# Sixteen norm roots taken with tokens on the partitions, in a two-block transformer on one Trainium2 core

## The reference

```python
def rms_norm(x, g):
    xf = x.astype(jnp.float32)
    y = xf * lax.rsqrt(jnp.mean(xf * xf, axis=-1, keepdims=True) + EPS)
    return (y * g.astype(jnp.float32)).astype(x.dtype)
```

```python
    x = x + rms_norm(mix, g_post_mix[i])
    ffn = conv_ffn(rms_norm(x, g_pre_ffn[i]), w_ffn_up[i], w_ffn_conv[i], w_ffn_down[i])
    x = x + rms_norm(ffn, g_post_ffn[i])
    x = x + per_layer_embed(x, p[i], g_pre_ple[i], w_ple_gate[i], w_ple_proj[i], g_post_ple[i])
```

## Time and profile before

| | |
|---|---|
| time, median of 3 runs (range) | 1460.56 us (1457.85 to 1463.82) |
| the profiled execution's own time | 1462.89 us |
| its span, first to last instruction | 1461.1 us |
| mean granted TensorE clock | 0.967 |
| PE busy | 1360.6 us (93%) |
| DVE busy | 909.1 us (62%) |
| ACT busy | 698.9 us (48%) |
| DMA | 205.22 MB, mean 140 GB/s |

### The profile page before, as it was taken

How to read it: one execution, slowest core, us unless ns; L and a number is a source line. 1 busy time by engine, 2 the same in 40 slices (tenths; PEclk the granted TensorE clock), 3 DMA queues, 4 the chain that set the end, 5 groups by cost and what they waited for, 6 DMA issues and landing times. The chain is left out here.

```text
span 1461.1 us, 24231 instructions
## 1 busy us (share of the span) xinstructions
PE 1360.6 (93%) x10604; PEld 1314.3 (90%) x10604; DVE 909.1 (62%) x1231; ACT 698.9 (48%) x1026; POOL 4.5 (0%) x13
## 2 busy tenths in 40 slices
PE   5898899999998999999998999998999898999994
PEld 4887689999998999999998999997898698999994
DVE  4578545665448565446557888465745557887465
ACT  4754133654333555334445655445534445556443
POOL 1000000000000000000000000000000000000000
PEclk9999979999999999999999999999899999999997
DMA  6132003555540455544541645532361033554520
GB/s 250 66 129 87 29 30 116 192 175 178 178 173 30 173 177 193 179 145 181 189 158 61 228 175 192 181 144 74 130 217 58 30 116 116 198 178 166 194 102 29
DMA packets 30906, 205.22 MB, mean 140 GB/s; under 512 B 3272, under 2 KB 5584, under 8 KB 7248
## 3 DMA queue, kind: packets, MB, share of 16 engines
q1 hardware_dynamic: 30800, 203.67, 39.5%
HBM read 202.59 MB, written 1.06 MB: 139 GB/s over the span
## 5 line engine op out<-in xcount | busy, mean ns | idle before, releaser
L309 DVE TENSOR_TENSOR WL<-RAW,WH 128x2048 fp32r<-128x2048 f32 (+2 forms) x192 | 432.7, 2257 | 334.1 <-ACT WH L302 333.9
L324 PE MATMUL PS<-UH,WH 128*128 128x256 f32 (+1 forms) x1624 | 468.6, 289 | 29.6 <-DVE WL L309 22.6
L302 ACT ACTIVATE WH<-RAW 128x2048 fp32r<-128x2048 f32 (+2 forms) x192 | 360.7, 1883 | 270.5 <-PE PS L324 270.5
L324 PE MATMUL PS<-UH,WL 128*128 128x256 f32 (+1 forms) x1624 | 467.3, 288 | 0.0
L324 PE MATMUL PS<-UL,WH 128*128 128x256 f32 (+1 forms) x1624 | 466.8, 287 | 0.0
L324 PEld LDWEIGHTS PS<-UH,WH 128*128 128x128 f32 x1624 | 313.8, 193 | 32.3 <-DVE WL L309 18.5
L324 PEld LDWEIGHTS PS<-UH,WL 128*128 128x128 f32 x1624 | 313.8, 193 | 0.0
L324 PEld LDWEIGHTS PS<-UL,WH 128*128 128x128 f32 x1624 | 312.4, 192 | 0.1
L324 PE MATMUL PS<-HL,WH 128*128 128x272 f32 (+1 forms) x512 | 145.8, 285 | 0.0
L324 PE MATMUL PS<-HH,WH 128*128 128x272 f32 (+1 forms) x512 | 145.6, 284 | 0.0
L324 PE MATMUL PS<-HH,WL 128*128 128x272 f32 (+1 forms) x512 | 145.4, 284 | 0.0
(11 more groups left out here) (373 smaller groups left out, 1962.5 us busy)
## 6 DMA issues: line engine op xcount, KB each, us to landing
RAW<-wpack SPq DMA_DIRECT2D x182, 1024.0 KB, 4.9
RAW<-wpack SPq DMA_DIRECT2D x9, 768.0 KB, 4.4
C<-cst SPq DMA_DIRECT2D x1, 1136.0 KB, 13.4
X<-xin SPq DMA_DIRECT2D x1, 1088.0 KB, 5.4
HB<-bias_rows SPq DMA_DIRECT2D x1, 1024.0 KB, 6.0
out<-X SPq DMA_DIRECT2D x4, 256.0 KB, 2.4
PI<-pin SPq DMA_DIRECT2D x2, 256.0 KB, 2.8
RAW<-wpack SPq DMA_DIRECT2D x1, 256.0 KB, 2.6
```

The lines of the kernel that those rows point to most:

```text
L302: a.e.activation(WH[n % NH][:, 0:w], RAW[n % NR][:, 0:w], ACT.Copy).then_inc(*a.mark("wh", n))
L309: v.e.tensor_tensor(WL[n % NH][:, 0:w], RAW[n % NR][:, 0:w], WH[n % NH][:, 0:w].bitcast(f32), ALU.subtract).then_inc(*v.mark("wl", n))
L324: ins = t.e.matmul(o, part(n, hw, kw, a, b), x(kx), start=first and not i and not p, stop=last and i == len(kcs) - 1 and p == 2)
```

## The change

Every root's sum is made with the squares as the stationary operand and one column of ones as the moving one, so that the results have tokens on the partitions: two columns of 128 tokens (in two banks) and, for 272 tokens, one of 16. Square root and reciprocal are taken on 128x2 values (and 16x1), kept in `RS`. `root_spread` brings them back: the root's column, broadcast to [n,128], is the stationary operand and an identity `ID` the moving one, which writes the 128x256 (272) values to the root's first bank. Users read them from PSUM (`spread`), and that bank is held until the last of them; for m, mlp0, mlp1, gate0, gate1 and kv ACT copies the bank to RR first (`root_keep`), and the users wait for that copy. Pair 3 of the squares is no longer added by DVE, but summed by PE from SQ[1]; `root_begin` sums ACC, `root_end` SQ[1]. In the outputs sco, do, f0, f1 root_begin stands between PE's last two groups of products. The ones products in six places of the code are fewer, the one-column products of m and kv are gone, and the identity is loaded at the start instead of with the constants.

```diff
+        ID = sb("ID", [128, 128])
+        RS = sb("RS", [128, 3 * len(ROOTED)])
...
-            a.free[slot] = ("acc", st, p) if p else ("sum", st)
+            a.free[slot] = ("acc", st, p) if p in (1, 2) else ("sum", st)
...
         def add_squares(v, st, i, p, w):
-            if p == 0:
+            if p not in (1, 2):
                 return
...
-        def root_sum(t, st, i, w):
-            t.wait_ge("acc", st, 3)
-            b = banks.take(t, ("root", st), ("rs", st))
-            t.e.matmul(PS[:, b, 0:w], ONE[:, :], ACC[i][:, 0, 0:w], start=True, stop=False)
-            t.e.matmul(PS[:, b, 0:w], ONE[:, :], ACC[i][:, 1, 0:w], start=False, stop=True).then_inc(*t.mark("sum", st))
+        def part_sum(t, b, x, a, z, src, m, first, last):
+            o = PS[0:z - a, b, 1:2] if x == 0 else PS[:, b + x - 1, 0:1]
+            return t.e.matmul(o, src[:, m, a:z], ONE[:, 0:1], start=first and m == 0, stop=last and m == 1)
+
+        def root_begin(t, st, i, w, freed):
+            b = banks.take(t, ("root", st), freed, 2)
+            banks.freed[b + 1] = ("rs", st)
+            t.wait_ge("acc", st, 2)
+            for x, (a, z) in token_blocks(w)[-2:]:
+                for m in range(2):
+                    part_sum(t, b, x, a, z, ACC[i], m, True, False)
+
+        def root_end(t, st, i, w):
+            b = banks.at["root", st]
+            for m in range(2):
+                t.wait_ge("sq", st, 3, m)
+                for x, (a, z) in token_blocks(w)[-2:]:
+                    ins = part_sum(t, b, x, a, z, SQ[1], m, False, True)
+            if w == T:
+                for src, first in ((ACC[i], True), (SQ[1], False)):
+                    for m in range(2):
+                        ins = part_sum(t, b, 0, 0, NM, src, m, first, not first)
+            ins.then_inc(*t.mark("sum", st))
...
+            a.e.activation(rooted(st, 1, 128, 2), PS[:, b:b + 2, 0], ACT.Sqrt, bias=EPS[:, 0:1], scale=1.0 / 1024).then_inc(
...
+            v.e.reciprocal(rooted(st, 1, 128, 2), rooted(st, 1, 128, 2)).then_inc(*v.mark("rr", st))
+
+        def root_spread(t, st, w):
+            b = banks.at["root", st]
+            t.wait_ge("rr", st)
+            t.wait_ge("id")
+            for x, (a, z) in token_blocks(w):
+                n = z - a
+                ins = t.e.matmul(PS[:, b, a:z], rooted(st, x, n).to_broadcast([n, 128]), ID[0:n, 0:n], start=True, stop=True)
+            ins.then_inc(*t.mark("rsp", st))
+
+        def root_keep(a, st, i, w):
+            a.wait_ge("rsp", st)
+            a.e.activation(RR[i][:, 0:w], spread(st, w), ACT.Copy).then_inc(*a.mark("rk", st))
...
+            s.e.dma_start(ID[:, :], cst[:, CAT["id"]:CAT["id"] + 128]).then_inc(*s.mark_dma("id"))
...
-            root_sum(t, "m", 0, T)
-            columns(0, RR[0], ("rr", "m"))
+            root_sum(t, "m", 0, T, ("rk", "m"))
+            root_spread(t, "m", T)
...
+                        if (uu, m) == (2, 0):
+                            root_spread(t, st, w)
...
             keep_going(t, 18)
-            root_sum(t, "pool", 0, T)
-            keep_going(t, 66)
+            root_sum(t, "pool", 0, T, ("py", 3, 1))
+            root_spread(t, "pool", T)
+            keep_going(t, 50)
...
+                        if (gg, bi, m) == (3, len(blocks) - 1, 0):
+                            root_begin(t, st, 1, S, freed)
...
             keep_going(t, 24)
-            root_sum(t, "sc", 0, S)
-            keep_going(t, 30)
+            root_sum(t, "sc", 0, S, ("uu", "sc", 3))
+            root_spread(t, "sc", S)
+            keep_going(t, 12)
...
-            tensor_output(t, "mix", "sco", lambda k: OH_[:, k, :], lambda k: OL_[:, k, :], lambda k: ("ol", k))
+            tensor_output(t, "mix", "sco", ("mr", "ffn0", 3), lambda k: OH_[:, k, :], lambda k: OL_[:, k, :], lambda k: ("ol", k))
...
             embed(0, 2)
-            root_sum(t, prev, 1, S)
-            embed(2, 4)
-            embed(4, 6)
-            keep_going(t, 52)
-            root_sum(t, st, 0, S)
-            embed(6, 8)
-            keep_going(t, 24)
+            root_end(t, prev, 1, S)
+            embed(2, 3)
+            root_spread(t, prev, S)
+            embed(3, 6)
+            keep_going(t, 36)
+            root_sum(t, st, 0, S, ("uu", st, 3))
+            embed(6, 7)
+            root_spread(t, st, S)
+            embed(7, 8)
+            keep_going(t, 12)
...
-            root_sum(t, f"f{layer}", 1, S)
-            keep_going(t, 42)
+            root_end(t, f"f{layer}", 1, S)
+            root_spread(t, f"f{layer}", S)
+            keep_going(t, 20)
...
+                        if (u, m) == (2, 1):
+                            root_spread(t, st, S)
...
-            root_sqrt(a, st, 0, S)
+            root_sqrt(a, st, S)
+            root_keep(a, st, 0, S)
             preload(a, ACT.Sigmoid)
...
-            root_sum(t, "ple0", 1, S)
-            keep_going(t, 54)
+            root_sum(t, "ple0", 1, S, ("mr", "kv", 3))
+            root_spread(t, "ple0", S)
+            keep_going(t, 28)
...
-            root_sum(t, "kv", 0, S)
-            b = banks.take(t, ("rkv",), ("rkv",))
-            t.wait_ge("rr", "kv")
-            for i in range(2):
-                ins = t.e.matmul(PS[:, b, i:i + 1], RR[0][0:1, 128 * i:128 * i + 128], c2("id", 1)[:, 0:1], start=True,
-                                 stop=True)
-            ins.then_inc(*t.mark("dif", "rkv"))
+            root_sum(t, "kv", 0, S, ("rk", "kv"))
...
+                    if j == 5:
+                        root_spread(t, "kv", S)
```

More of the change, by code:

```diff
@@ L275, in program @@
         SM = sb("SMALL", [128, 64])
+        ID = sb("ID", [128, 128])
+        ROOTED = ("m", "mlp0", "pool", "mlp1", "sc", "sco", "ffn0", "f0", "gate0", "ple0", "kv", "do", "ffn1", "f1",
+                  "gate1", "ple1")
+        RS = sb("RS", [128, 3 * len(ROOTED)])
         PS = ctx.enter_context(nc.psum_tensor("PS", [128, 8, 512], f32))
@@ new lines, in root_sum, with root_sqrt @@
+        def root_sum(t, st, i, w, freed):
+            root_begin(t, st, i, w, freed)
+            root_end(t, st, i, w)
+        def root_sqrt(a, st, w):
+            b = banks.at["root", st]
+            a.wait_ge("sum", st)
+            if w == T:
+                a.e.activation(rooted(st, 0, NM), PS[0:NM, b, 1:2], ACT.Sqrt, bias=EPS[0:NM, 0:1], scale=1.0 / 1024)
+            a.e.activation(rooted(st, 1, 128, 2), PS[:, b:b + 2, 0], ACT.Sqrt, bias=EPS[:, 0:1], scale=1.0 / 1024).then_inc(
+                *a.mark("rs", st))
@@ new lines, in root_recip @@
+        def root_recip(v, st, w):
+            v.wait_ge("rs", st)
+            if w == T:
+                v.e.reciprocal(rooted(st, 0, NM), rooted(st, 0, NM))
+            v.e.reciprocal(rooted(st, 1, 128, 2), rooted(st, 1, 128, 2)).then_inc(*v.mark("rr", st))
+        def root_spread(t, st, w):
+            b = banks.at["root", st]
+            t.wait_ge("rr", st)
[4 more added lines that the diff above has]
+            ins.then_inc(*t.mark("rsp", st))
@@ L398, in preload, with spread @@
+        def spread(st, w):
+            return PS[:, banks.at["root", st], 0:w]
+        def root_keep(a, st, i, w):
+            a.wait_ge("rsp", st)
+            a.e.activation(RR[i][:, 0:w], spread(st, w), ACT.Copy).then_inc(*a.mark("rk", st))
         def preload(a, func):
@@ L1240, in scalar_mlp @@
                 if uu == 0:
[L1241 removed]
+                    root_sqrt(a, st, w)
+                    root_keep(a, st, 1, w)
                     preload(a, ACT.Square)
@@ L1323, in scalar_pool @@
             preload(a, ACT.Sqrt)
-            root_sqrt(a, "pool", 0, T)
+            root_sqrt(a, "pool", T)
             for gi in range(4):
@@ L1418, in scalar_output @@
                             a.wait_ge(*a.free[slot])
-                        a.free[slot] = ("acc", st, p) if p else ("sum", st)
+                        a.free[slot] = ("acc", st, p) if p in (1, 2) else ("sum", st)
                     src = PS[:, banks.at[st, j], 0:S]
-                    ins = a.e.activation(dst[:, m, 0:S], src, ACT.Square)
-                    if m:
-                        ins.then_inc(*a.mark("sq", st, p))
+                    a.e.activation(dst[:, m, 0:S], src, ACT.Square).then_inc(*a.mark("sq", st, p, m))
+                    sig.also(("sq", st, p), ("sq", st, p, m))
                     a.e.activation(M[:, j, :], src, ACT.Copy, scale=g(name, j)).then_inc(*a.mark("m", st, j))
@@ L1461, in enter_vector @@
             if prev is not None:
-                root_recip(v, prev, 1, S)
-            rm = both(RR[1][:, 0:S])
+                root_recip(v, prev, S)
+            rm = both(spread(prev, S)) if prev is not None else None
             def low(j, src):
@@ L1489, in enter_vector @@
                     fill()
-                root_recip(v, st, 0, S)
-                v.wait_ge("rr", st)
-                rr = both(RR[0][:, 0:S])
+                root_recip(v, st, S)
+                v.wait_ge("rsp", st)
+                rr = both(spread(st, S))
```

(5 more changed lines are left out.)

112 lines of the change are left out of this document (55 added, 57 removed).

## The result

The changed kernel takes 1482.73 us, median of 4 runs (1480.17 to 1484.82), against 1459.38 (1457.85 to 1463.82) in the same comparison: ratio 1.0154, 95% interval 1.0123 to 1.0186, slower by 18 to 27 us. Forecast were 1478 and a range of 1460 to 1486. The profiled executions stand 17.85 us apart in span, 1479.0 against 1461.1, where the sum of the prediction said 17.6.

The account below looks back on a forecast made before the run. PE, busy in 93% of the span, was taken to bound the kernel, so only its waits, ones products and lower clock give time. The terms summed to +17.6 us on the median 1460.56: 1478 us, range 1460 to 1486.

Parts of the forecast that it names:

- Roots whose chain is waited for: Outputs f0 and f1, sc, pool, end: a shorter root chain saves 1.6 us each at f0 and f1, 3.0 at the rest.
- rival 5: PSUM operands cost DVE 65 ns each after all, in 44 instructions, some 2.8 us: 1481 us; chance 0.03.
- pool: In pool, where the next input waits for the root: a shorter root chain, −0.85 us.
- ffn's entries: At ffn0 and ffn1, banks held by roots stop PE's ones products and first products: +3.3 and +3.0 us.
- Late spreads: MLPs and gates: spread behind group (2,0) makes the users late; mlp0 +4.2 us, mlp1 +2.2, gates +2.9 each.
- rival 4: The clock falls at each longer wait and stays low for long, gates too: +24 us or more, 1486; chance 0.05.
- kv: In kv, the root's copy holds up XH, WH and WL, PE idles 5 us and the clock falls: +3.5 us.
- kv's entry: At kv's entry: 16 records at half speed against 4, one DMA fewer, a shorter reciprocal: +0.7 us.
- Rival 1: At ffn's entries the bank wraps don't bite and both terms become −1: 1470 us; chance 0.12.
- rival 2: In MLPs, gates and kv late spreads are free: 1454 us without ffn's bank wraps, 1462 with them; chance 0.14.
- rival 3: Late spreads free but ffn's bank wraps real, or half of the late spreads hidden: near 1464 us; chance 0.08.
- rival 6: root_begin is held up by the add before it, which takes back −3.2 us: 1481 us; chance 0.03.

Follow-up runs that it names:

- r6: The kernel before, wide roots kept, with one weight unit's split moved ahead of the root's users in MLPs, gates and kv: 1447.82 us, ratio 0.9911.
- r1: The changed kernel with ffn's entry ones products writing the root's second bank instead of taking one from the cycle: 1472.81 us, ratio 1.0104.
- r2: The changed kernel with the spread behind 9 products of the next group instead of 24, in MLPs, gates and kv: 1467.76 us, ratio 1.0068.
- r3: The changed kernel with the Sigmoid table load ahead of the root's copy to SBUF in the gates: 1483.56 us, ratio 1.0177.
- after: First profile of the changed kernel, unaltered: span 1479.0 us.
- again: Second profile of the same changed kernel, unaltered, from the first experiment: span 1474.9 us; that experiment's median 1482.23 us, ratio 1.0167.
- r9: The changed kernel with the one-column products on ACC made six more times in the sums of mlp0 and mlp1: 1502.02 us, ratio 1.0291.
- r4: The changed kernel with the edits of r1, r2 and r3 together: 1456.75 us, ratio 0.9986 to the kernel before.
- r5: r4 plus one weight unit's split moved ahead of the root's users in MLPs, gates and kv: 1447.55 us, ratio 0.9901 to the kernel before.
- r7: The changed kernel with wide roots back in both MLPs and both gates, ffn's banks and kv's spread mended: 1454.92 us, ratio 0.9968.
- r8: The changed kernel with wide roots in the MLPs only, the edits of r1 and r3, early spreads in gates and kv, r5's split ahead: 1440.77 us, ratio 0.9884.

## Why the prediction was right, and where it was not

**Roots whose chain is waited for: right.** −1.9 at f0 and f1 for −1.6, −1.1 for sc, −0.9 at the end. Of the −1.9 the chain gave 1.45, at the first unit behind the root. M·RR began 4.67 behind PE's last product at f0 before, and 2.38 after, with 0.88 of sum put ahead of that product:

```profile
989.00 0.17 DVE L438 RECIPROCAL RS<-RS 128x2 f32<-128x2 f32 x1 [2.19 <-ACT RS L431]
989.97 0.69 DVE L1539 TENSOR_TENSOR M<-M,PS 128x512 f32<-128x512 f32 x1 [0.80 <-PE PS L446]
```

The other 0.5 came a little per unit ahead of it: the down products of ffn (operands FH, FL, at full clock) follow each other every 117.3 ns, and did every 118.3. The products of the queries (XH, XL) in attention likewise: 113.7 ns for 120.0 over the first two units, which is most of a steady 0.9 of attention's −1.4. All ten profiles with the change show the shorter steps, and neither of the two without it (before, r6) does. The prediction had no term for this 1.9 in all; what causes it, the place of the operands in SBUF or something else, was not tried.

The prices (instructions by line, ns min/median/max; then the sum on PE in mlp0):

```profile
L431 ACT ACTIVATE RS<-PS,EPS x16: 237/262/264, 14.8 to 1469.0; 128x2 f32<-128x2 f32 x16
...
L438 DVE RECIPROCAL RS<-RS x16: 133/166/169, 15.2 to 1469.3; 128x2 f32<-128x2 f32 x16
...
L454 ACT ACTIVATE RR<-PS x6: 384/384/398, 17.2 to 1446.9; 128x256 f32<-128x256 f32 x4, 128x272 f32<-128x272 f32 x2
...
L1539 DVE TENSOR_TENSOR M<-M,PS x16: 677/680/687, 777.8 to 1433.2; 128x512 f32<-128x512 f32 x16
```
```profile
253.32 0.95 PE L399 MATMUL PS<-ONE,ACC 128*128 128x1 f32 x8
254.13 1.03 PE L399 MATMUL PS<-ONE,SQ 128*128 128x1 f32 x8
255.09 0.25 PE L399 MATMUL PS<-ONE,ACC 128*16 128x1 f32 x4
255.20 0.24 PE L399 MATMUL PS<-ONE,SQ 128*16 128x1 f32 x4
```

Reciprocal and copy as charged (0.17, 0.38), the sum 2.05 from first start to the next product for 1.97, the square root 262 ns where the nearest row had 172. M·RR with the root in PSUM takes 680 ns, with RR in SBUF it took 681 to 693, so rival 5 is out. The Trainium skill's fixed cost for a PSUM operand ("VectorE: DVE Perf Modes", the section on the TRN2 errata, 120 cycles against 58 from SBUF) is not seen here either. By that page's figures, an estimate, it would be some 65 ns more, 750.

**pool: wrong by 1.05.** +0.2 for −0.85. Two square roots one behind the other (16x1, then 128x2) took 0.40 where I had 0.22, and the granted clock fell behind the sum: DVE began on the spread root 1.66 after the spread's first record (450.56, 452.22) where I had 0.88 (the stretch of the sum, then that of the spread):

```profile
448.00:450.60 2.60, 1.86 (x23) 1.76 (x23) 0.21 (x2) 0.40 (x2) 0.00 (x0) 1.00 0.06 19
450.80:454.20 3.40, 3.40 (x17) 3.36 (x17) 1.91 (x4) 0.00 (x0) 0.00 (x0) 0.51 0.00 0
```

**ffn's entries: right in place and in kind.** The idle of 2.89 and 3.21 behind ("mr", 3) and the first product behind UUf, +3.9 in ffn0. r1 gives back 2.5 and 3.3. But the table has only +0.2 for do and ffn1 (forecast +3.0): the kernel before had a low stretch of 6.9 us at 1163 to 1170, among four waits that the kernel after has too (2.35 the longest, in both), and the changed kernel had none in either profile (stretch of before, as above):

```profile
1163.20:1170.10 6.90, 5.46 (x26) 5.46 (x27) 3.92 (x7) 2.48 (x2) 0.00 (x0) 0.51 0.01 2
```

That is a draw of the clock and not an effect of the change: r2 and r3, which are the changed kernel in this stage, have it (1171.4 to 1178.2, 1178.5 to 1185.3), and there the row is +4.2 in both. Of the twelve profiles nine have a low stretch here; only after, again and r1 do not. So the small row is the lucky one: with such a stretch in the changed kernel's profile too, the table would add up to some 22, and the medians say 23.

**Late spreads: right, mlp0 too low.** gates +2.8 for +2.9 each. In that sum the table load counted 1.48 less the 0.79 that DVE's two products took before as well, 0.69; r3 shows 0.51. mlp1 +1.3 for +2.2: what followed in the stage gave 0.5 back, and the clock's low stretch was as long as before. mlp0 +4.8 to +7.1 for +4.2. The step that failed there is "a fall in mlp0, at 1.5": there were two stretches, the first (256.2 to 259.6) right behind the sum:

```profile
253.30:255.40 2.10, 2.10 (x27) 2.06 (x25) 0.00 (x0) 0.00 (x0) 0.00 (x0) 1.00 0.00 0
256.20:259.60 3.40, 3.40 (x17) 3.40 (x16) 0.00 (x0) 0.00 (x0) 0.00 (x0) 0.50 0.00 0
```

PE is busy for all of 2.10 us there, and the clock falls nonetheless. r9 shows what neither the sum nor rival 4 had: one-column products keep PE busy and let its clock fall all the same. I had priced only the time that they take. That the same is at work in a sum of usual length is argued, not shown: behind mlp0's it fell in four of seven profiles (after, r1, r2, r4; not again, r3, r5), behind mlp1's in none, and behind the wide sum in mlp0 in none of four (before, r6, r7, r8).

**kv: right in mechanism, 1.5 low.** The chain keep, XH, WH, WL is as described; ACT's XH starts only when the copy is done:

```profile
1065.45 0.38 ACT L454 ACTIVATE RR<-PS 128x256 f32<-128x256 f32 x1 [3.13 <-PE PS L446]
1065.73 0.50 ACT L462 ACTIVATE XH<-X,G 128x256 fp32r<-128x256 f32 x1
```

and of the row's 5.1, 2.7 stand at the end of the WL that PE waits for, for the 2.2 forecast. The mis-sized part is the clock: PE's wait of 5.05 was followed by 6.8 us at the lower clock, and they cost 2.3 where the sum had left 1.3.

**kv's entry: wrong by 2.3.** The term had "one DMA fewer" without a size; before, PE waited 1.79 for exactly the constants behind it, and this wait is gone (waits of before):

```profile
PE PS L1938 <- DMA C<-cst: 1.8, 1, 1.8
```

It is at the edge of being met: in r9, which leaves this stage as it is, the constants took 4.8 us to land for 3.0, a wait of 1.54 stands there again, and the row is +0.8 for −1.6.

**The sum.** 17.6 forecast, 17.9 in the profiles, 23 in the medians. That is closer than the terms deserve, and is luck in good part: errors of mlp0 (+2.9), kv (+1.5), pool (+1.1) and layer 0's draw (+2.4) were met by kv's entry (−2.3), mlp1 (−0.9), ffn1's draw (−2.8) and attention (−1.4, of which 0.9 are the shorter steps of its products). The bounds were also added up wrongly by 1 each: the low ends give +9, not +10, and the high ends +25, not +24; no chance hangs on it. Rival 1 is out (r1), rival 2 is out (r2, r7), rival 3, a time near 1464, is out with them, rival 6 is out (f0). Rival 4 held in small part: the low stretches at mlp0 and kv are longer than forecast, but the total is not +24.

## What to carry to other kernels

Ask of each use of a value whether the next stage waits for it or whether PE's own work covers it: a shorter chain pays only in the first kind, and in the second whatever it adds to PE, or puts in front of the weights' preparation, is paid in full; here the first kind got some 6 us (outputs, sc, end), the second lost 17 to 19 (MLPs, gates, kv), and the held banks another 6 by the stages that r1 mended (9 by its median). A PSUM bank held for a reader is a wait for whoever comes round the cycle, fillers included: walk through the cycle once. And where PE waits for weights, look first at what stands ahead of their preparation in the other engines' programs: one unit moved ahead of the root's users gave 12 us (r6) without any new arithmetic.

## What the runs showed of the hardware that I had not expected

- Products with one moving column count as busy PE, but the granted clock falls to 0.50 during them: within the sum in both MLPs of r9 (PE busy 3.5 of 3.5 us before it, without a gap), and right behind a sum of 2.05 us in mlp0 of the changed kernel (in four of seven profiles).
- Whether the clock falls at a wait of some 3 us differs between executions of one kernel: both profiles of the changed kernel have a wait of 3.1 to 3.2 us that ends at 69.4 to 69.7, and the low stretch at 68.5 to 75.3 stood in one of them alone. Their spans were 1479.0 and 1474.9.
- PE's steps between products of one shape are not fixed, even at full clock: 256-column products of the queries came every 120.0 ns before and every 113.7 after, in the same code.
- A square root of 128x2, one column from each of two banks and with a bias, took 262 ns; the ACT instruction on two adjacent columns of one bank that I priced it by took 172. That row is no root, as its heading calls it, but an exponential (L2052). Which of the differences costs the 90 ns was not tried.
